# Stick-breaking attention in a two-part block: scores masked once, read straight from the projections, in an unrolled pipeline

## What is computed

```python
def one_block(args):
    q_blk, blk = args
    z = jnp.einsum('bhqd,bhkd->bhqk', q_blk, k).astype(jnp.float32) * scale
    q_pos = blk * BLOCK + jnp.arange(BLOCK)
    valid = (key_pos[None, :] < q_pos[:, None]) & (key_pos[None, :] >= PAD)
    log_1m = jnp.where(valid, jax.nn.log_sigmoid(-z), 0.0)
    log_after = lax.cumsum(log_1m, axis=3, reverse=True) - log_1m
    w = jnp.where(valid, jnp.exp(jax.nn.log_sigmoid(z) + log_after), 0.0)
    return jnp.einsum('bhqk,bhkd->bhqd', w.astype(v.dtype), v)
```

## Time and profile before

| | us |
|---|---|
| median of 3 runs | 1558.01 (1553.12 to 1563.17) |
| the profiled execution | 1562.59 |
| its span in the trace | 1560.8 |
| PE busy in the span | 1466.6 (94%) |
| DVE busy | 897.8 (58%) |
| ACT busy | 328.3 (21%) |
| POOL busy | 32.0 (2%) |
| stick stage, from the end of L1484 to the last L1730 | 92.1 |

### The profile page before, as it was taken

The page is one execution under the profiler, slowest core; times in us unless marked ns, Lnnn a source line. Parts: engine busy times, 40 slices in busy tenths (PEclk is TensorE's granted clock), DMA queues, the critical chain, the costliest instruction groups (busy, mean ns, idle before and its releaser), DMA issues.

```text
span 1560.8 us, 30115 instructions
## 1 busy us (share of the span) xinstructions
PE 1466.6 (94%) x12742; PEld 1322.8 (85%) x12742; DVE 897.8 (58%) x1783; ACT 328.3 (21%) x657; POOL 32.0 (2%) x47
## 2 busy tenths in 40 slices
PE   7999999989999969998889999999998889999997
PEld 6888788889999836777787999989998778999997
DVE  2141133347864481466554777886685546887865
ACT  1132104140000111420112122220101652222201
POOL 0130000000000000000000000000001100000000
PEclk9999999999999989999998999999998668999999
DMA  8434244246544402321000344444443002444442
GB/s 338 152 122 158 68 148 149 97 126 205 176 174 163 162 0 99 118 70 42 4 4 2 112 139 155 162 146 173 169 162 135 1 1 96 147 162 152 147 163 81
DMA packets 54479, 190.42 MB, mean 122 GB/s; under 512 B 6961, under 2 KB 9137, under 8 KB 53970
## 3 DMA queue, kind: packets, MB, share of 16 engines
q1 hardware_dynamic: 50480, 180.67, 33.7%
q10 hardware_dynamic: 3874, 7.92, 1.6%
HBM read 187.51 MB, written 1.05 MB: 121 GB/s over the span
## 4 chain that ended last, share of the span: by engine, by line
PE 87%; DVE 8%; issue 3%; ACT 1%; DMA 0%; POOL 0%; DVEq 0%; ACTq 0%; SPq 0%; PEldq 0%; POOLq 0%
PE ps L1799 86%; DVE arena L1551 1%; DVE arena L1574 1%; DVE arena L1602 1%; DVE arena L1717 0%; DMA ring<-in_stream 0%; DVE rs L2255 0%; DVE arena L1601 0%; DVE arena L792 0%; DVE arena L1721 0%; DVE arena L790 0%; DVE arena L1340 0%; DVE arena L1332 0%; DVE res L2264 0%; DVE arena L1330 0%
## 5 line engine op out<-in xcount | busy, mean ns | idle before, releaser
L1799 PE MATMUL ps<-arena,ring 128*128 128x136 f32 (+3 forms) x4816 | 864.0, 333 | 18.0 <-DMA ring<-in_stream 8.1
L1799 PEld LDWEIGHTS ps<-arena,ring 128*128 128x128 f32 x4816 | 752.0, 193 | 103.1 <-issue 19.9
L1799 PE MATMUL ps<-arena 64*64 64x64 f32 (+8 forms) x6748 | 572.0, 263 | 45.9 <-DVE arena L1730 12.2
L1799 PEld LDWEIGHTS ps<-arena 64*64 64x64 f32 (+3 forms) x6748 | 504.1, 165 | 88.0 <-issue 44.6
L790 DVE TENSOR_TENSOR arena<-ring 128x512 f32<-128x512 f32 x92 | 63.3, 688 | 95.1 <-PE ps L1799 93.6
L1799 PE MATMUL ps<-arena,consts 128*128 128x16 f32 (+10 forms) x384 | 90.4, 391 | 8.5 <-DVE arena L1721 4.8
L1551 DVE SCALAR_TENSOR_TENSOR arena<-arena,cols 128x271 f32<-128x271 f32 (+1 forms) x176 | 84.0, 498 | 11.2 <-ACT arena L1226 8.1
L1799 PEld LDWEIGHTS ps<-arena,consts 128*128 128x128 f32 (+3 forms) x384 | 70.5, 231 | 22.2 <-DVE arena L1721 4.9
L777 ACT COPY arena<-ps 128x136 f32<-128x136 f32 (+1 forms) x64 | 17.2, 268 | 323.1 <-PE ps L1799 323.1
L1226 ACT ACTIVATE arena<-arena,cols 128x272 f32<-128x272 f32 x88 | 49.2, 606 | 125.0 <-DVE arena L1484 70.3
L792 DVE TENSOR_TENSOR arena<-arena,ring 128x512 f32<-128x512 f32 x92 | 63.7, 693 | 3.2
(11 more groups left out here) (270 smaller groups left out, 896.6 us busy)
## 6 DMA issues: line engine op xcount, KB each, us to landing
ring<-in_stream SPq DMA_DIRECT2D x342, 512.0 KB, 3.7
consts<-in_consts ACTq DMA_DIRECT2D x1, 1580.0 KB, 8.7
arena<-in_x_t ACTq DMA_DIRECT2D x1, 1024.0 KB, 5.8
arena<-in_mem_t ACTq DMA_DIRECT2D x1, 1024.0 KB, 4.8
res<-in_x_t ACTq DMA_DIRECT2D x1, 1024.0 KB, 14.6
out_t<-arena SPq DMA_DIRECT2D x4, 256.0 KB, 2.5
arena<-in_g ACTq DMA_DIRECT2D x1, 640.0 KB, 5.8
arena<-in_w ACTq DMA_DIRECT2D x2, 256.0 KB, 4.7
```

What stands on the lines that cost most here:

```text
L1799: return nc.tensor.matmul(out, lhs, rhs, start=start, stop=stop)
```

## The change

It rewrites the stick stage in these points:

- No staging: POOL's copies, their buffers, the memsets and `k_staged` go. TensorE reads `kT`, `qT`, `vT` directly; the last key tile is 16 wide everywhere, so its products have 16 stationary rows or columns.
- The scores are scaled and masked once, by VectorE, into `zs` (five instructions, as before) as soon as the scores are there; Abs and the maximum both read `zs`, so that the 0/1 mask at L1721 goes. ScalarE starts a unit after VectorE's scaling.
- The copy of the transposed values goes from ScalarE to VectorE. VectorE's turn becomes: scaling and maximum of t, copy of the values of t, copy of the output of t - 2, suffix sum of t - 1, `ll` of t.
- TensorE makes the scores ahead of the transposes.
- `ee` is three deep.
- The ten turns are unrolled on all engines, with waits on constants.
- Products whose result nothing reads (`keep_busy`, 240 columns each, into unused columns of bank 6): ten behind the scores of unit 1, four ahead of the output of units 6 and 7.

Apart from the declarations of the semaphores and the call of POOL's part, the diff is this:

```diff
--- before.py
+++ after.py
@@ -481,11 +481,11 @@
         four = Space(arena, width)
         ZW = L + (L - P) + META
 
-        kst, vs2, qst = four.take(2, 384), four.take(2, 384), four.take(2, L)
-        zs, ll, ee = [[four.take(2, ZW) for _ in range(2)] for _ in range(3)]
+        zs, ll, ee = [[four.take(2, ZW) for _ in range(n)] for n in (2, 2, 3)]
         vk2 = four.take(2, 3, P)
         assert four.at <= KT * L * 2 + 4 * L + F2 * L
         ZC = [0, L, L + L - P]
+        KW = [P, P, META]
 
         for name in ("upq", "rw_r", "rw_k", "rw_v", "lora", "exp_kk", "exp_rk", "rw_o", "ffa_up", "ffa_down",
                      "sb_k", "sb_v", "sb_q", "sb_o", "ffb_up", "ffb_down"):
@@ -728,7 +723,8 @@
             pe.sem_inc(ev["sb_q"], GB)
             seven_products(pe, mm, "sb_q", lambda: pe.wait_ge(ev["sb_v"], GB + 8))
             pe.wait_ge(ev["sb_q"], GB + 8)
-            stick_units(pe, lambda t, it: stick_tensor(pe, mm, t, it))
+            for t in range(KT + 2):
+                stick_tensor(pe, mm, t)
             pe.wait_ge(k_od, KT)
             pe.sem_inc(ev["sb_o"], GB)
             tiles("sb_o", FIRST["sb_o"], 2, oT, L)
@@ -1064,67 +1060,60 @@
             spread_a(2)
             spread_a(3)
 
-        def stick_units(eng, turn):
-
-            turn(0, None)
-            turn(1, None)
-            with eng.Fori(0, 2) as it:
-                turn(2, it)
-                turn(3, it)
-            for t in range(6, 10):
-                turn(t, None)
-
-        def unit(eng, s, u, it):
-
-            if u >= 0:
-                eng.wait_ge(s, u + 1 if it is None else it * 2 + (u + 1))
-
-        def z_products(pe, mm, u, it):
+        def keep_busy(pe, mm, n):
+            for _ in range(n):
+                mm(ps[:, 6, L:512], const("ones"), consts[:, 0:512 - L])
+
+        def z_products(pe, mm, u):
             b = u % 2
-            unit(pe, k_staged, u, it)
-
-            unit(pe, k_vk, u - 1, it)
-            unit(pe, k_zr, u - 2, it)
-            for n in range(3):
-                last = nc.tensor.transpose(ps[:, 7, n * P:(n + 1) * P], vs2[:, b, n * P:(n + 1) * P], ident)
-            last.then_inc(k_vt, 1)
+            if u >= 2:
+                pe.wait_ge(k_zr, u - 1)
             for i in range(3):
                 for p in range(2):
                     r = slice(64 * p, 64 * p + 64)
-                    last = mm(ps[:, 2 * b + p, ZC[i]:ZC[i] + L - i * P], kst[r, b, i * P:(i + 1) * P],
-                              qst[r, b, i * P:L])
+                    last = mm(ps[0:KW[i], 2 * b + p, ZC[i]:ZC[i] + L - i * P], kT[r, u, i * P:i * P + KW[i]],
+                              qT[r, u, i * P:L])
             last.then_inc(k_z, 1)
-
-        def stick_tensor(pe, mm, t, it):
+            if u == 1:
+                keep_busy(pe, mm, 10)
+            if u >= 1:
+                pe.wait_ge(k_vk, u)
+            for n in range(3):
+                last = nc.tensor.transpose(ps[0:KW[n], 7, n * P:(n + 1) * P], vT[:, u, n * P:n * P + KW[n]], ident)
+            last.then_inc(k_vt, 1)
+
+        def stick_tensor(pe, mm, t):
+            u, b = t - 1, (t - 1) % 2
             if t == 0:
-                z_products(pe, mm, 0, it)
-            if 1 <= t <= 8:
-
-                u, b = t - 1, (t - 1) % 2
-                unit(pe, k_l, u, it)
-                unit(pe, k_arg, u - 1, it)
+                z_products(pe, mm, 0)
+            if 0 <= u < KT:
+                pe.wait_ge(k_l, u + 1)
+                if u >= 1:
+                    pe.wait_ge(k_arg, u)
                 for e in range(2):
                     for i in range(3):
-                        last = mm(ps[:, 4 + e, ZC[i]:ZC[i] + L - i * P], const("after"),
-                                  ll[b][:, e, ZC[i]:ZC[i] + L - i * P], True, i == 2)
+                        last = mm(ps[:, 4 + e, ZC[i]:ZC[i] + L - i * P], const("after")[0:KW[i], :],
+                                  ll[b][0:KW[i], e, ZC[i]:ZC[i] + L - i * P], True, i == 2)
                         for j in range(i + 1, 3):
                             w = L - j * P
                             last = mm(ps[:, 4 + e, ZC[i] + (j - i) * P:ZC[i] + (j - i) * P + w],
-                                      const("ones"), ll[b][:, e, ZC[j]:ZC[j] + w], False, j == 2)
+                                      const("ones")[0:KW[j], :], ll[b][0:KW[j], e, ZC[j]:ZC[j] + w], False, j == 2)
                 last.then_inc(k_sfx, 1)
-            if t + 1 <= 7:
-                z_products(pe, mm, t + 1, it)
-            if 1 <= t <= 8:
-                unit(pe, k_w, u, it)
-                unit(pe, k_vk, u, it)
-                unit(pe, k_od, u - 1, it)
+            if t + 1 < KT:
+                z_products(pe, mm, t + 1)
+            if 0 <= u < KT:
+                pe.wait_ge(k_vk, u + 1)
+                if u >= 1:
+                    pe.wait_ge(k_od, u)
+                if u >= KT - 2:
+                    keep_busy(pe, mm, 4)
+                pe.wait_ge(k_w, u + 1)
                 for i in range(3):
                     for p in range(2):
                         r = slice(64 * p, 64 * p + 64)
-                        last = mm(ps[r, 6, i * P:L], vk2[:, b, i, r], ee[b][:, p, ZC[i]:ZC[i] + L - i * P],
-                                  i == 0, i == 2)
+                        last = mm(ps[r, 6, i * P:L], vk2[0:KW[i], b, i, r],
+                                  ee[u % 3][0:KW[i], p, ZC[i]:ZC[i] + L - i * P], i == 0, i == 2)
                 last.then_inc(k_o, 1)
-
 
         def load_lora(act):
             for dst, src in ((w1s, w1_d), (a1s, a1_d), (g1s, g1_d), (w2s[0:64, :], w2_d), (a2s[0:64, :], a2_d),
@@ -1197,7 +1186,8 @@
             for name in ("sb_k", "sb_v", "sb_q"):
                 for i in range(SEVEN[name].i0, 4):
                     keep_first_product(act, name, i)
-            stick_units(act, lambda t, it: stick_scalar(act, f, t, it))
+            for t in range(KT + 2):
+                stick_scalar(act, f, t)
             residual_scalar(act, f, "sb_o", ("ffn_g", 8), seven=1)
             ffn_scalar(act, f, root, "ffb", 1, 12)
             residual_scalar(act, f, "ffb_down", ("fin_g", 0), seven=0)
@@ -1295,24 +1285,20 @@
             f(y_sq[:, :, PART_B], ps[:, 0, :].rearrange("p (n t) -> p n t", n=KT), ACT.Square).then_inc(y_act.sem, 1)
             root("b", PART_B)
 
-        def stick_scalar(act, f, t, it):
-            if t <= 7:
-                u, b = t, t % 2
-
-                unit(act, k_vt, u, it)
-                unit(act, k_o, u - 2, it)
-                nc.scalar.copy(vk2[:, b], ps[:, 7, 0:3 * P].rearrange("p (a b) -> p a b", a=3)).then_inc(k_vk, 1)
-
-                unit(act, k_z, u, it)
-                f(ee[b], ps[:, 2 * b:2 * b + 2, 0:ZW], ACT.Abs, scale=0.125).then_inc(k_abs, 1)
-                unit(act, k_abs, u, it)
-                f(ee[b], ee[b], ACT.Exp, scale=-1.0).then_inc(k_exp, 1)
-                unit(act, k_exp, u, it)
-                f(ee[b], ee[b], ACT.Ln, bias=one_c).then_inc(k_ln, 1)
-            if 1 <= t <= 8:
-                u, b = t - 1, (t - 1) % 2
-                unit(act, k_arg, u, it)
-                f(ee[b], zs[b], ACT.Exp).then_inc(k_w, 1)
+        def stick_scalar(act, f, t):
+            if t < KT:
+                e = ee[t % 3]
+                act.wait_ge(k_zr, t + 1)
+                if t >= 3:
+                    act.wait_ge(k_o, t - 2)
+                f(e, zs[t % 2], ACT.Abs).then_inc(k_abs, 1)
+                act.wait_ge(k_abs, t + 1)
+                f(e, e, ACT.Exp, scale=-1.0).then_inc(k_exp, 1)
+                act.wait_ge(k_exp, t + 1)
+                f(e, e, ACT.Ln, bias=one_c).then_inc(k_ln, 1)
+            if 1 <= t <= KT:
+                act.wait_ge(k_arg, t)
+                f(ee[(t - 1) % 3], zs[(t - 1) % 2], ACT.Exp).then_inc(k_w, 1)
 
 
         def second_vector(dve, link, v, tt, stt, ts, inverse_root, residual, normed_to, take):
@@ -1505,10 +1491,9 @@
             dve.wait_ge(hq_scaled, 1)
             x_sums(link, tt, "sb_q")
             seven_vector(dve, tt, "sb_v", lambda i: quads_scaled("sb_v", i, vT[:, 2 * i:2 * i + 2, :]), then="sb_q")
-            v.memset(kst[:, :, L:384], 0.0)
-            v.memset(vs2[:, :, L:384], 0.0).then_inc(zeroed, 1)
             seven_vector(dve, tt, "sb_q", lambda i: quads_scaled("sb_q", i, qT[:, 2 * i:2 * i + 2, :]))
-            stick_units(dve, lambda t, it: stick_vector(dve, t, it, v, tt, stt, ts, cpv))
+            for t in range(KT + 2):
+                stick_vector(dve, t, tt, stt, ts, cpv)
             dve.wait_ge(k_od, KT)
             x_sums(link, tt, "sb_o")
             weight_sums(dve, tt, "sb_o", 1, 0)
@@ -1692,69 +1677,39 @@
             variance("a", 7, PART_A, TA)
             inverse("a", PART_A)
 
-        def stick_vector(dve, t, it, v, tt, stt, ts, cpv):
-            diag = [(ZC[i], min(P, L - i * P)) for i in range(3)]
-            rest = [(P, L), (L + P, L + P + META)]
-            if t <= 7:
-
-                b = t % 2
```

(86 more changed lines are left out.)

10 lines of the change are left out of this document (3 added, 7 removed).

## The result

| | before | after |
|---|---|---|
| median of the comparison | 1560.38 us (1551.56 to 1565.49, 11 runs) | 1550.87 us (1543.03 to 1556.65, 11 runs) |
| ratio, with its 95% interval | | 0.9949 (0.9925 to 0.9972) |
| the profiled execution | 1562.59 | 1547.31 |
| stick stage with its last output copy | 92.5 | 79.5 |
| of it at half clock | 65.2 | 20.5 |

The change makes the kernel about 0.5% faster, some 8 us, about half of what was forecast; the median lies in the range of 1532 to 1556, but above the 1547 that the likeliest case allowed. The two profiled executions lie 15.3 us apart, nearly the 17.3 of the sum.

A forecast was written before the change was run, and what follows sets the result against it. The stage was taken as a latency loop over TensorE and VectorE, with TensorE often at half clock. First pair no gain, then 8.1 us cycles: 14.3 plus 3.0 gives 17.3 us, median 1541 us, range 1532 to 1556.

The forecast's parts named there:

- the likeliest case: Whole kernel: median 1541 us, by itself 1535 to 1547; chance 0.50.
- the sum: Whole kernel: 14.3 us sooner at the stage's last output copy plus 3.0 in the output projection, together 17.3 us.
- First pair: Start of the stick stage: pair 0's weights ready at 1220.6 against 1220.16 before, so no gain.
- The cycle: Stick stage, one pair's weights to the next: 8.1 us instead of 10.1, by latency and TensorE's work; ScalarE's loop 7.8.
- The second rival: Stick stage: shape changes cost nothing, the clock is up early and ScalarE's 7.8 us binds; 1537 us, chance 0.13.
- Changes of shape at 0.20 each: TensorE, narrow last tile: fourteen array-shape changes a unit instead of three, 0.20 us each, making the suffix 4.9 us.
- Dearer: Rival on TensorE's shape changes: 0.30 us each, suffix 5.6, cycle 8.9, whole kernel 1547 us; chance 0.19.
- Output projection at full clock, 3.0 us: Behind the stick stage: the projection ran 6.0 us at half clock, takes 3.0 at full, gaining 3.0 us.
- The step that failed: TensorE in the stick stage: hardly idle at 8.1 us a pair, so its clock stays full from the ten products on.
- its last rival: Stick stage: clock falls once behind the first pair and stays at half for all pairs; 55 us more, 1596 us; chance 0.09.
- a few pairs at half: Stick stage: some pairs at half clock take 15.6 us each, 7.5 more than at full; two give 1556 us; chance 0.09.
- All pairs at half: Stick stage: every pair after the first at half clock, 55 us more, 1596 us; chance 0.09.

The follow-up runs named there:

- before_unread2: The kernel before plus only unread products: ten behind the second scores, six a pair ahead of the output; 1545.88 us, ratio 0.9923 to before.
- no_abs: The kernel after without ScalarE's Abs, its Exp reading the scaled scores times 0.001 (other values result); 1535.88 us, ratio 0.986 to before.
- wide: The kernel after with the last key tile 128 wide again in all products; 1538.65 us, ratio 0.9894 to before.
- no_unread: The kernel after without any of its unread products; 1552.48 us, ratio 0.9965 to before.
- first_fill: The kernel after plus five unread products between pair 1's transposes and pair 0's suffix; 1544.25 us, ratio 0.9919 to before.
- again5: The kernel after, unedited, run again for a sixth profile; 1556.2 us, ratio 0.9981 to before, stage 87.6 us.

## Why the prediction was off

The sum was 17.3 us of gain, the gain 7.2 (all executions) to 9.5 (the medians of the comparison). The sign and many of its terms held; the clock did not, and it was half of the mechanism.

- **First pair** (weights at 1220.6, 19.9 us into the stage; "gains nothing"): 18.1 to 19.0 in the six profiles of after, 18.2 to 19.5 in the five of before. That it gains nothing is right, partly by luck. The forecast had TensorE, not ScalarE, hold the first suffix up, to 13.0 us into the stage. In the profile of after it starts at 9.2, and as it then runs at half (7.71 instead of 4.9) the two errors nearly cancel. At full clock the first pair is 2.5 us slower than the old one, by before_unread2.
- **The cycle.** "8.1 us, with TensorE hardly idle": at full clock 7.89, set by ScalarE with the 7.8 that the prediction worked out for it, and TensorE waits 0.80 us a pair, more than the 0.5 that the prediction named as a sign of it. The second rival was right on this. The loop through TensorE came out at 7.75, where 8.1 was forecast, because a change of shape costs less. TensorE's own work, also forecast at 8.1, is 7.1 in no_abs; the transposes were mis-sized most (1.05 forecast; 0.55 at full clock in the timeline of after).
- **Changes of shape at 0.20 each.** Suffix 4.48 instead of 4.9: (4.48 - 3.5)/7 = 0.14 at full clock, 0.15 against `wide`. At half clock (7.99 - 6.48)/7 = 0.22. The time mix's row was a good bound, and a third too high. "Dearer" is wrong.
- **Maximum 0.6, copy of the values at most 0.62**: 0.61 and 0.55, hidden. Right. POOL, the memsets, the loops: as said, nothing seen of them.
- **Output projection at full clock, 3.0 us**: 264.6 against 267.3 behind the stage on average, 2.6; in the first pair of profiles 3.0. Right; the one profile of no_unread, with 266.6, speaks for the unread products ahead of the last outputs as its cause.
- **The step that failed** is "with TensorE hardly idle, and that is what keeps its clock", with "clock 1.0 from the ten products on". TensorE was busy 92% of the stage and the clock was at half for 20 to 37 us of it in every profile of after. Two things let it fall. One is idle time in pair 0: 1.1 to 1.9 us ahead of its suffix in four of the six profiles, where the forecast had TensorE busy until after the suffix was due (it priced the ten unread products partly at half clock), and 3.0 us ahead of its weights in five. The prediction had the second wait, with up to 2 us, as the condition of its last rival, and gave that 0.09; cutting it to 0.96 us (the profile of first_fill) went with some 6 us less. The other is the suffix of narrow products itself, where the clock fell with TensorE busy 3.20 of 3.20 us, 14 times in the ten profiles with such a tile and never in the ten without; the earlier trace rows had shown a dense stretch of 16-row products ahead of a half clock, and the prediction set that aside by one window of 6.6 us.
- **What it costs.** A stage of after wholly at full clock would take some 18.1 + 6 x 7.89 + 7.66 + 1.7 = 74.8 us, an estimate from the parts of several profiles, 3.4 under the forecast's 78.2. The average stage is 83.5. So 28 us at half clock cost 8.7, and the forecast missed the stage by 5.3. The rival "a few pairs at half" has the right mechanism with a pair too dear: 15.6 us forecast, where the three pairs that ran at half from end to end took 12.1 to 12.5. The changes of shape were put at 0.4 each in it and cost 0.22. "All pairs at half" did not happen: in the profiles of after the clock came back within 3 to 17 us.
- **The base.** The sum stood against a profile of 1562.6. The mean of all executions of before is 1558.1. The prediction named the difference to the median, 4.6 us, and left it outside the stage. Against the mean of the five profiles of before this one has 0.5 us more ahead of the stage, 0.7 in it and 0.3 behind it; the other 3.0 lie between the profiled executions and all executions and are not placed.

Together: 17.3, less 0.7 for a stage of before that was above the average (92.5 against 91.8), less 5.3 for the stage of after, nearly all of it clock, less 0.4 behind it, comes to 10.9, the 11.0 of the averaged profiles. To the 7.2 of all executions 3.8 are left open.

The Trainium skill (TensorE: Matmul & The Clock Gate, section HAM oscillation) names idle time of the engine as what lets the clock fall. The fall in a wait of 3.06 us agrees with it in kind; the falls with TensorE busy for 3.40 of 3.40 us, and the 16.70 us fully busy at half behind one, don't. The same skill (TensorEngine Tiling (Array Packing), section Tiling Modes) says that a change of mode drains TensorE; the runs agree, with 0.14 to 0.15 us for each at full clock.

## What to carry to other kernels

Where the clock of a stage rises and falls, one profile of it is a draw, not the state of things: take several, and give the clock its own term with a price by the us at half (here 0.31 us lost for each). Look for the wait behind which the clock falls in most profiles, here the 3.0 us for pair 0's weights, and shorten that one first: in one profile five unread products cut it to 0.96 us, and some 6 us less went with them, nearly what the rebuilt pipeline had brought. Don't narrow a tile to save rows that cost nothing: 16 records of 272 columns take 3.83 us with 16 rows as with 128, and each change of shape is paid. Compare pipelines at the same clock before you rebuild one: here the old one at full clock has a stage of 77.5 us, against the estimated 74.8 of the new one, and its first pair is the faster.

## What the runs showed of the hardware

- TensorE's clock can fall from 2.4 to 1.2 GHz with the engine busy without a gap, behind a suffix in which half of the fp32 records have 16 rows (3.40 of 3.40 us busy, again5), and stay at half for 16.7 us of unbroken work. It came back sooner or later among the same products. With tiles of 128 in their place no fall came without idle time ahead of it, in ten profiles.
- A change of the array's shape costs 0.14 to 0.15 us at full clock and 0.2 at half. That is less than proportional to the clock.
- The same program takes from 1540 to 1557 us in one comparison, and nearly all of that goes with its mean granted clock (correlation -0.95).
